# A hybrid convolution, state-space and Fourier block: how the first token tiles are normalised and turned, and how the first quarter of the modulation matrix is loaded

## The chip, the cores and the metric

The kernel runs on one core of one Trainium2 chip. The metric is the device time of one execution in microseconds (us). Before the change three executions took 2059.18, 2054.16 and 2054.33 us; the median is 2054.33 us.

## The reference, cut to what matters

One layer over 512 latent tokens and 256 context tokens of width 2048. What the change touches is the beginning: the modulation vectors, the RMS norm, and the first projection of it.

```python
mod_x = jax.nn.silu(c) @ w_ada[l] + b_ada[l]              # w_ada is 2048 x 6144
sh_x, sc_x, gt_x = jnp.split(mod_x[:, None, :], 3, axis=-1)
mod_c = jax.nn.silu(c_ctx) @ w_ada[l] + b_ada[l]
sh_c, sc_c, gt_c = jnp.split(mod_c, 3)
h_x = _rmsnorm(x, g_pre[l]) * (1 + sc_x) + sh_x           # x is 512 x 2048
h_c = _rmsnorm(ctx, g_pre[l]) * (1 + sc_c) + sh_c         # ctx is 256 x 2048
parts_x = _split_proj(h_x @ w_in[l])                      # w_in is 2048 x 14336
u_c = h_c @ w_in[l][:, U_OFF:U_OFF + W_SSM]
```

All of it is float32. The convolution branch, the state-space scan, the Fourier branch, the gates and the output projection follow from `parts_x` and `u_c` and are the same before and after.

## The kernel before, in words

The kernel is written out by hand for each engine, with semaphores between them; every engine works its list in order. After a head of some 160 us it is a long run of matrix products on TensorE. Float32 matrices are split into a rounded high part and a low part (ScalarE copies the high part, VectorE subtracts), and each product is high by high, high by low and low by high.

A piece of `w_in` in the long run is 128 columns wide, so its row pieces are 512 B.

The head computes `h_x` and `h_c`, transposed (channels on the partitions), and the first four column blocks of the `u` projection. It loads on the queue of SyncE, in this order (lines 378 to 387): the two condition rows, x in four tiles of 128 tokens (1 MB each), then 32 units of `w_ada`, 1 MB each as two transfers of 512 KB (line 367), through a ring of four places. Unit n waits until unit n - 4 has been used. Behind units 6 and 7 of each eight comes one 512 KB unit of `w_in` (line 374), and behind units 8 and 9 one tile of ctx each. The 32 units are four quarters of eight: quarter q holds columns 512q to 512q + 511 of the shift part and of the scale part, all 2048 rows, 256 rows in each unit. A row piece of a unit is 2 KB long.

TensorE, per quarter: `ada` (line 586) multiplies a unit by the two condition vectors and accumulates two short rows in PSUM; after eight units ScalarE copies the rows out (`rows_cp`, line 989), `cols` (line 593) turns them to columns and VectorE's `columns` (line 1434) forms scale and shift for four blocks of 128 channels. VectorE's `modulate` (lines 1452 and 1456) applies them to a turned block, ScalarE's `high` and VectorE's `low` (line 1465) split the result. `x_piece` (lines 633 to 637) and `c_piece` (650 to 653) are the products of one block with its part of `w_in`. The first `ada` of a quarter waits for `columns` of the quarter before (`col_rd`), since both use one PSUM bank.

The norm of the latent tokens (lines 1010 to 1022): ScalarE squares and sums the four tiles, one square root serves all four, VectorE finishes the reciprocal root (lines 1362 and 1354 to 1358), and ScalarE scales all four tiles in place. Then TensorE turns twelve of the sixteen channel blocks (`early_turn`, line 602, four transposes of 128x128 each) in groups of three between `ada` units 3 to 6, and ScalarE copies each to `xT`. The other four blocks are turned in the last quarter. The ctx tiles are squared, scaled and turned later (lines 1027 to 1034 and 620).

VectorE has a second job in the head: the discretisation of the state-space part, on small tiles [128, 64]. It is an exponential of one column (starting at line 1346) and of 64 (1348), the steps for the sine (lines 1366 to 1383), for the cosine (1387 to 1391), `zoh` (1395 to 1409) and `chunk_powers` (1412 to 1425). In the first quarter `zoh` stands ahead of the ctx blocks' `modulate`, and `chunk_powers` behind them, ahead of `columns(1)`.

Of the kernel before, what the change touches and what calls it, by code (L numbers as in the profile page):

```python
# [28 lines left out]
D = 2048  # L29
T = 512  # L30
# [69 lines left out]
def program(nc, x, c, ctx, c_ctx, w_ada, b_ada, g_pre, g_post, w_in, conv_w, lam_re, lam_im, log_dt,  # L100
# [15 lines left out]
    class Region:  # L116
# [5 lines left out]
        def __call__(self, name, shape, dt=F32):  # L122
# [71 lines left out]
    junk = at("junk", [128, D], abr_at + KD // 2 * TC * 4)  # L194
    last4 = (KD - 4) * T * 4
    ring = [at(f"ring{n}", [128, 2, 2, 512], off)
            for n, off in enumerate((hx_at + last4, hxl_at + last4, tab_at, tab_at + 8192))]
# [25 lines left out]
    vrow = r("vrow", [V_END, 128])  # L223
    lam = r("lam", [128, 2, P])
# [3 lines left out]
    assert r.p <= abr_at + KD // 2 * TC * 4  # L228
# [60 lines left out]
                            for name, n in (("ada_in", 4), ("u_out", 4), ("gw_in", 4)))  # L289
# [34 lines left out]
    win = lambda col, n: [(w_in, 0, col, n), (w_in, 1024, col, n)]  # L324
    ph_u = (2, lambda i: [q for j in range(2) for q in win(COL["u"] + 512, (i, 2, j))])
# [245 lines left out]
    def _(pe):  # L571
# [6 lines left out]
        def ada(n):  # L578
            q, r = n // 8, n % 8
            if r == 0 and q:  # L580
                pe.wait_ge(col_rd, q)
            pe.wait_ge(ada_in[n % 4], 32 * (n // 4 + 1))
# [7 lines left out]
        def cols(q):  # L590
            pe.wait_ge(row_cp, q + 1)
            for k in range(4):
# [4 lines left out]
        def early_turn(k):  # L597
            pe.wait_ge(y_done, TT)
            if k >= 4:
                pe.wait_ge(xp_done, k - 3)  # L600
            for t in range(TT):
                last = tr(ac[:, k % 4, t * 128:(t + 1) * 128], xn[:, t, k * 128:(k + 1) * 128], ident[:, :])
            last.then_inc(xp_ps, 1)

        def turn(q, n):
# [4 lines left out]
            if n < 4:  # L610
                pe.wait_ge(y_done, TT)
# [70 lines left out]
        for n in range(8):  # L682
            ada(n)
            if n == 3:
                pe.wait_ge(vec_in, 64)
                tr(ss[:, 1, 0:V_END], vrow[:, :], ident[0:V_END, 0:V_END])
                tr(ss[:, 1, 128:128 + G], drow[:, :, :].rearrange("n l h -> n (l h)"), ident[0:G, 0:G]).then_inc(vec_ps, 1)
            if 3 <= n < 7:
                for k in range(3 * (n - 3), 3 * (n - 2)):
                    early_turn(k)  # L690
        cols(0)
        ada(8)
        ada(9)
        pe.wait_ge(xp_done, EARLY)
        for r in range(4):
            x_piece(0, r, range(4))
            ada(10 + r)
        turn(0, 4)
        ada(14)
        turn(0, 5)  # L700
        for q in range(3):
            if q:
                x_piece(q, 0, range(4))
                ada(8 * q + 12)
                x_piece(q, 1, range(4))
                turn(q, 4)
                ada(8 * q + 13)
                x_piece(q, 2, range(4))
                ada(8 * q + 14)
                turn(q, 5)  # L710
                x_piece(q, 3, range(4))
# [258 lines left out]
    def _(act):  # L970
# [19 lines left out]

        def high(q, n):
# [18 lines left out]
        for t in range(TT):  # L1010
            act.wait_ge(x_in[t], 16)
            st.link(a(junk[:, :], toks[t], ACT.Square, accum_out=small[:, 32 + t:33 + t]))
        act.wait_ge(var_done, 1)
        a(small[:, 46:50], small[:, 40:44], ACT.Sqrt).then_inc(rt_done, 1)
        act.wait_ge(rs_done, 1)
        for t in range(TT):
            cp(toks[t], toks[t], small[:, 52 + t:53 + t]).then_inc(y_done, 1)
        for k in range(EARLY):
            act.wait_ge(xp_ps, k + 1)
            cp(xT[:, k, :], ac[:, k % 4, :]).then_inc(xp_done, 1)  # L1020
            if k == 8:
                hi_first(0)
        hi_first(1)
        rows_cp(0)
        for n in range(4):
            high(0, n)
# [3 lines left out]
        act.wait_ge(var_done, 2)  # L1030
        a(small[:, 50:52], small[:, 44:46], ACT.Sqrt).then_inc(rt_done, 1)
        act.wait_ge(rs_done, 2)
# [264 lines left out]
        act.wait_ge(var_done, 3)  # L1297
# [9 lines left out]
    def _(dve):  # L1307
# [4 lines left out]
        st.link(v.memset(ss[:, 2, :], 0.0))  # L1312
# [30 lines left out]
        dve.wait_ge(ssm_in, 48)  # L1343
        a0, a1, a2, a3, a4, a5, a6, a7 = [z[:, :] for z in zt]
        lre, lim = lam[:, 0, :], lam[:, 1, :]
        exp(a7[:, 0:1], ldt[:, :], a1[:, 0:1], a2[:, 0:1], a3[:, 0:1], a4[:, 0:1], ei[:, 0:1])
        link(ts_(a0, lre, a7[:, 0:1], None, ALU.mult))
        exp(a6, a0, a1, a2, a3, a4, ei[:, :])

# [16 lines left out]
        link(ts_(a0, lim, a7[:, 0:1], None, ALU.mult))  # L1366
        nearest(a1, a0, 1.0 / math.pi)
        link(stt(a2, a1, -3.140625, a0, ALU.mult, ALU.add))
        link(stt(a2, a1, -9.67502593994140625e-4, a2, ALU.mult, ALU.add))
        link(stt(a2, a1, -1.509957990978376432e-7, a2, ALU.mult, ALU.add))  # L1370
        nearest(a3, a1, 0.5)
# [593 lines left out]
```

## Time and profile before

| what | value |
|---|---|
| median of three executions | 2054.33 us |
| the profiled execution's own time | 2054.32 us |
| its span, first to last instruction | 2052.5 us |
| TensorE busy | 2008.0 us, 98% of the span |
| TensorE weight loads | 1640.1 us, 80% |
| VectorE busy | 1085.8 us, 53% |
| ScalarE busy | 594.9 us, 29% |
| data moved | 270.72 MB, 132 GB/s over the span |

Matrix products are pipelined, so a product's duration (392 ns for one of 512 columns) is longer than the step from one to the next. Positions in time below are microseconds from the start of the span. In a row of the timeline the first number is the start, the second the length of the whole group, and the bracket at the end the idle time of the engine just before it and what ended it. A float32 product that isn't a transpose is recorded as two instructions.

### The profile page before, as it was taken

The numbers are of one execution on the slowest core, as the hardware profiler recorded it, in microseconds if no ns is written. First come the engines' busy times: TensorE is split into PE (matmuls) and PEld (weight loads), VectorE is DVE, ScalarE is ACT, GpSimd is POOL, SyncE is SP. The second block draws the span as 40 slices with busy tenths as digits, with TensorE's granted clock in tenths as the row PEclk, the third lists the DMA queues.
The fourth block names the chain that finished last, engine by engine and source line by source line (L and its number), as shares of the span: only waits on it lengthen the run. The fifth ranks groups of instructions, "written<-read, shape, count | busy, mean of one in ns | idle before, by whom it ended". The sixth has DMA issues, their size and how long they took to land.

```text
span 2052.5 us, 26821 instructions
## 1 busy us (share of the span) xinstructions
PE 2008.0 (98%) x10086; PEld 1640.1 (80%) x10086; DVE 1085.8 (53%) x1640; ACT 594.9 (29%) x845; POOL 27.4 (1%) x16
## 2 busy tenths in 40 slices
PE   4999999999999999999999999999999999999998
PEld 1568888888888888888888888888888888888886
DVE  4545799999998645554433434332433333333325
ACT  5325343334343322222222222222322222222222
POOL 0003100000000000000000000000000000000000
PEclk9999999999999999999999999999999999999999
DMA  9963544344344544443334444443233333334423
GB/s 361 366 199 116 168 106 109 102 106 108 102 108 112 179 129 133 125 138 108 100 94 138 134 123 138 133 133 104 73 92 102 93 97 97 93 101 154 173 99 128
DMA packets 384079, 270.72 MB, mean 132 GB/s; under 512 B 24820, under 2 KB 349916, under 8 KB 382164
## 3 DMA queue, kind: packets, MB, share of 16 engines
q1 hardware_dynamic: 373728, 265.61, 42.0%
q10 hardware_dynamic: 10292, 4.33, 1.5%
q8 instruction: 36, 0.59, 0.1%
q14 instruction: 23, 0.19, 0.0%
HBM read 251.81 MB, written 18.09 MB: 131 GB/s over the span
## 4 chain that ended last, share of the span: by engine, by line
PE 93%; DVE 3%; ACT 2%; DMA 1%; issue 1%; SPq 0%; ACTq 0%; DVEq 0%
PE ac L753 25%; PE ac L757 25%; PE ac L754 24%; PE ac L938 1%; PE ac L939 1%; PE ac L937 1%; PE ss L815 1%; PE ss L586 1%; PE ss L939 1%; PE ss L938 1%; PE ss L937 1%; PE ac L633 1%; PE ac L634 1%; PE ac L637 1%; DMA wslot<-w_in 1%; PE ss L808 1%
## 5 line engine op out<-in xcount | busy, mean ns | idle before, releaser
L1557 DVE TENSOR_TENSOR wlo<-wslot,whi 128x1024 fp32r<-128x1024 f32 x309 | 378.3, 1224 | 643.4 <-ACT whi L973 639.3
L973 ACT ACTIVATE whi<-wslot 128x1024 fp32r<-128x1024 f32 x327 | 346.9, 1061 | 1244.3 <-PE ac L757 1042.8
L753 PE MATMUL ac<-hxh,whi 128*128 128x512 f32 x1664 | 651.9, 392 | 0.0
L754 PE MATMUL ac<-hxl,whi 128*128 128x512 f32 x1664 | 647.8, 389 | 0.0
L757 PE MATMUL ac<-hxh,wlo 128*128 128x512 f32 x1664 | 411.2, 389 | 0.9 <-DVE wlo L1557 0.9
L753 PEld LDWEIGHTS ac<-hxh,whi 128*128 128x128 f32 x1664 | 312.4, 188 | 67.4 <-issue 2.9
L757 PEld LDWEIGHTS ac<-hxh,wlo 128*128 128x128 f32 x1664 | 312.3, 188 | 66.1 <-DVE wlo L1557 1.3
L754 PEld LDWEIGHTS ac<-hxl,whi 128*128 128x128 f32 x1664 | 312.4, 188 | 63.8
L753 PE MATMUL ac<-bah,whi 128*128 128x512 f32 x384 | 149.4, 389 | 0.0
L754 PE MATMUL ac<-bal,whi 128*128 128x512 f32 x384 | 149.4, 389 | 0.0
L757 PE MATMUL ac<-bah,wlo 128*128 128x512 f32 x384 | 94.8, 389 | 0.0
L753 PEld LDWEIGHTS ac<-bah,whi 128*128 128x128 f32 x384 | 72.1, 188 | 15.0
L757 PEld LDWEIGHTS ac<-bah,wlo 128*128 128x128 f32 x384 | 72.1, 188 | 15.0
L754 PEld LDWEIGHTS ac<-bal,whi 128*128 128x128 f32 x384 | 72.1, 188 | 14.9
L753 PE MATMUL ac<-b2nd,whi 128*128 128x512 f32 x192 | 74.8, 390 | 0.0
L754 PE MATMUL ac<-b2nd,whi 128*128 128x512 f32 x192 | 74.7, 389 | 0.0
L1776 DVE TENSOR_TENSOR gtm<-ac,gsig 128x512 f32<-128x512 f32 x32 | 22.1, 691 | 85.7 <-PE ac L757 85.7
L586 PE MATMUL ss<-ring,cs 128*2 128x512 f32 x256 | 38.0, 675 | 24.0 <-DMA ring<-w_ada 20.7
L1732 DVE SCALAR_TENSOR_TENSOR gacc<-gwt,cs,gacc 128x256 f32<-128x256 f32 x120 | 57.8, 481 | 3.4
L937 PE MATMUL ac<-whi,mhi 128*128 128x512 f32 x128 | 50.2, 392 | 0.0
L939 PE MATMUL ac<-whi,mlo 128*128 128x512 f32 x128 | 49.8, 389 | 0.0
L938 PE MATMUL ss<-wlo,mhi 128*128 128x512 f32 x128 | 49.8, 389 | 0.0
(359 smaller groups left out, 2076.0 us busy)
## 6 DMA issues: line engine op xcount, KB each, us to landing
wslot<-w_in SPq DMA_DIRECT2D x224, 512.0 KB, 3.8
ring<-w_ada SPq DMA_DIRECT2D x64, 512.0 KB, 8.4
gwt<-w_ada SPq DMA_DIRECT2D x128, 128.0 KB, 2.5
wslot<-w_out SPq DMA_DIRECT2D x32, 512.0 KB, 3.6
wslot<-proj_a SPq DMA_DIRECT2D x16, 512.0 KB, 4.1
wslot<-proj_b SPq DMA_DIRECT2D x16, 512.0 KB, 4.1
wslot<-proj_c SPq DMA_DIRECT2D x16, 512.0 KB, 3.9
xn<-x SPq DMA_DIRECT2D x4, 1024.0 KB, 9.6
```

Source lines behind the costliest of these rows:

```text
L586: last = mm(ss[p:p + 2, 2, :], cs[:, 2 * r + kk, :], ring[n % 4][:, kk, h, :], start=(r == 0), stop=(r == 7))
L633: mm(ac[:, m, :], w, hxh[:, k, :], start=(k == 0), stop=False)
L753: mm(ac[:, bank, :], w, xh, start=(v == 0 and q == 0), stop=False)
L754: mm(ac[:, bank, :], w, xl, start=False, stop=False)
L757: last = mm(ac[:, bank, :], wlo[:, s, q * 128:(q + 1) * 128], rhs(v * UNIT + q)[0], start=False, stop=(v == nu - 1 and q == UNIT - 1))
L937: mm(acc[:, t, :], mh, wh, start=(kk == 0), stop=False)
L938: mm(acc[:, t, :], mh, wl, start=False, stop=False)
L939: last = mm(acc[:, t, :], ml, wh, start=False, stop=(kk == KD - 1))
L973: cp = lambda o, i, scale=1.0: nc.scalar.activation(o, i, ACT.Copy, scale=scale)
L1557: tt(wlo[:, s, :], wslot[:, s, :], whi[:, (U0[k] + j) % 2, :].bitcast(F32), ALU.subtract)\
L1732: stt(gacc[:, :], gwt[:, r % 4, :], cs[:, r, 0:1], gacc[:, :], ALU.mult, ALU.add)\
L1776: tt(o if br == 0 else gtm2[:, :], ac[:, (2 * j + 1) % 4, :], gsig[:, :], ALU.mult)\
```

## The change

The latent tiles are no longer scaled in place. For each tile VectorE makes a diagonal matrix of its 128 reciprocal roots as soon as that tile's sum is there, and TensorE multiplies the raw tile by it, which scales and turns at once (a float32 product in place of a transpose). Root and reciprocal are done per tile. The twelve blocks of one tile are three PSUM banks of four blocks, in rotation over five banks. The remaining four channel blocks are scaled in place by ScalarE, behind the ctx tiles.

The first quarter of `w_ada` is loaded in two halves of its columns: unit n below 8 holds 512 rows of 256 columns, so that four units complete the first half; a row piece is 1 KB. Two ring places are added, used once each. `cols`, `columns` and the row copy of the first quarter are done per half. The first two `w_in` units come behind units 3 and 7, both ctx tiles behind unit 7. The order of the first quarter on TensorE, ScalarE and VectorE is written anew; sine, cosine and `zoh` move behind other work of VectorE.

```diff
+    diag = at("diag", [128, TT, 128], abr_at + L * H * 4)
+            for n, off in enumerate((hx_at + last4, hxl_at + last4, tab_at, tab_at + 8192,
+                                     hx_at + 4 * T * 4, hx_at + 8 * T * 4))]
+    slot = lambda n: n if n < 6 else (n - 6 if n < 8 else n % 4)
...
SyncE, ada_unit(n)
-            if n >= 4:
-                sp.wait_ge(ada_used, n - 3)
+            if n >= 6:
+                sp.wait_ge(ada_used, n - 3 if n > 9 else n - (5 if n < 8 else 1))
+            if n < 8:
+                half, r = n // 4, n % 4
+                for h in range(2):
+                    sp.dma_start(halves(n)[:, :, h, :],
+                                 w_ada[r * 512:(r + 1) * 512, h * D + half * 256:h * D + (half + 1) * 256]
+                                 .rearrange("(k p) c -> p k c", p=128)).then_inc(ada_in[slot(n)], 16)
+                return
...
         for n in range(32):
             ada_unit(n)
-            if n % 8 >= 6:
+            if n in (3, 7):
+                first_unit(n // 4)
+            if n == 7:
+                for t in range(CT):
+                    sp.dma_start(cn[:, t, :], ctx[0, t * 128:(t + 1) * 128, :]).then_inc(c_in, 16)
+            if n > 8 and n % 8 >= 6:
                 first_unit(n // 8 * 2 + n % 2)
-            if n in (8, 9):
-                sp.dma_start(cn[:, n - 8, :], ctx[0, (n - 8) * 128:(n - 7) * 128, :]).then_inc(c_in, 16)
...
TensorE
+        def early_turn(t):
+            pe.wait_ge(y_done, t + 1)
+            for g in range(PARTS):
+                n = t * PARTS + g
+                if n >= 5:
+                    pe.wait_ge(xp_done, n - 4)
+                for k in range(4):
+                    c0 = (4 * g + k) * 128
+                    last = mm(early_bank(n)[:, k * 128:(k + 1) * 128], xn[:, t, c0:c0 + 128], diag[:, t, :],
+                              start=True, stop=True)
+                last.then_inc(xp_ps, 1)
...
+        early_turn(0)
+        early_turn(1)
+        early_turn(2)
+        ada(0)
+        early_turn(3)
+        for n in range(1, 4):
             ada(n)
+        pe.wait_ge(vec_in, 64)
+        tr(ss[:, 1, 0:V_END], vrow[:, :], ident[0:V_END, 0:V_END])
+        tr(ss[:, 1, 128:128 + G], drow[:, :, :].rearrange("n l h -> n (l h)"), ident[0:G, 0:G]).then_inc(vec_ps, 1)
+        cols(0, range(2))
+        ada(4)
+        ada(5)
+        pe.wait_ge(xp_done, TT * PARTS)
+        x_piece(0, 0, range(4))
+        ada(6)
+        ada(7)
+        x_piece(0, 1, range(4))
+        cols(0, range(2, 4))
         ada(8)
         ada(9)
+        x_piece(0, 2, range(4))
+        ada(10)
+        x_piece(0, 3, range(4))
         turn(0, 4)
+        ada(11)
+        turn(0, 5)
+        ada(12)
+        c_piece(0, 0)
+        ada(13)
         ada(14)
+        c_piece(0, 1)
+        ada(15)
+        c_piece(0, 2)
+        cols(1)
+        c_piece(0, 3)
+        for n in range(16, 20):
+            ada(n)
(quarters 1 to 3 as before)
...
ScalarE
+        token_square(0)
+        token_root(0)
+        token_square(1)
+        token_root(1)
+        token_square(2)
+        token_root(2)
+        early_out(0)
+        token_square(3)
+        token_root(3)
+        for t in range(1, TT):
+            early_out(t)
+        rows_half(0)
+        hi_first(0)
+        high(0, 0)
+        high(0, 1)
+        rows_half(1)
         hi_first(1)
+        high(0, 2)
+        high(0, 3)
         act.wait_ge(c_in, 32)
...
         for t in range(TT, TT + CT):
             cp(toks[t], toks[t], small[:, 52 + t:53 + t]).then_inc(y_done, 1)
+        for t in range(TT):
+            o = xn[:, t, EARLY * 128:]
+            last = cp(o, o, small[:, 52 + t:53 + t])
+        last.then_inc(y_done, 1)
         high(0, 4)
...
VectorE
+        def token_diag(t):
+            token_scale(t, 1, t + 1)
+            dve.wait_ge(rs_done, t + 1)
+            ts_(diag[:, t, :], ident[:, :], small[:, 52 + t:53 + t], None, ALU.mult).then_inc(y_done, 1)
+        token_diag(0)
+        token_diag(1)
+        dve.wait_ge(ssm_in, 48)
+        exp(a7[:, 0:1], ldt[:, :], a1[:, 0:1], a2[:, 0:1], a3[:, 0:1], a4[:, 0:1], ei[:, 0:1])
+        token_diag(2)
+        token_diag(3)
...
         for q in range(4):
+            columns(q, range(2 if q == 0 else 4))
+            modulate(q, 0)
             if q == 0:
                 lo_first(0)
-            columns(q)
-            modulate(q, 0)
             low(q, 0)
             modulate(q, 1)
             low(q, 1)
-            if q:
+            if q == 0:
+                sines()
+                columns(0, range(2, 4))
+            else:
                 lo_first(2 * q)
             modulate(q, 2)
+            if q == 0:
+                lo_first(1)
             low(q, 2)
             modulate(q, 3)
             low(q, 3)
-            lo_first(2 * q + 1)
-            if q == 0:
-                token_scale(TT, CT, 2)
-                zoh()
+            if q:
+                lo_first(2 * q + 1)
+            else:
+                token_scale(TT, CT, TT + 1)
             for n in range(4, 6):
                 modulate(q, n)
                 low(q, n)
             if q == 0:
+                cosines()
+                zoh()
                 chunk_powers()
```

## Rows read from the trace of the kernel before

**Rows 1.** The page, busy time of each engine.

```profile
PE 2008.0 (98%) x10086; PEld 1640.1 (80%) x10086; DVE 1085.8 (53%) x1640; ACT 594.9 (29%) x845; POOL 27.4 (1%) x16
```

**Rows 2.** Stretches of the head: busy time per engine, granted clock, DMA share, GB/s.

```profile
49.00:52.00 3.00, 2.46 (x10) 0.66 (x11) 1.61 (x4) 1.26 (x2) 0.00 (x0) 0.50 1.00 386
...
79.00:84.00 5.00, 4.57 (x36) 2.70 (x37) 3.54 (x9) 2.21 (x3) 0.00 (x0) 1.00 0.63 201
80.00:100.00 20.00, 20.00 (x128) 11.95 (x121) 8.93 (x15) 5.05 (x7) 0.00 (x0) 1.00 0.94 339
100.00:120.00 20.00, 20.00 (x134) 12.83 (x134) 8.39 (x15) 5.73 (x8) 0.00 (x0) 1.00 0.94 328
```

**Rows 3.** The DMA view of the stretch from 17 to 76 us.

```profile
DMA packets 11106, 22.99 MB, mean 390 GB/s; under 512 B 669, under 2 KB 669, under 8 KB 10847
```

**Rows 4.** The timeline of TensorE, 0 to 150 us.

```profile
18.94 1.89 PE L586 MATMUL ss<-ring,cs 128*2 128x512 f32 x8 [15.50 <-DMA ring<-w_ada]
...
31.43 2.82 PE L602 MATMUL ac<-ident,xn 128*128 128x128 f32 x12 [1.00 <-ACT xn L973]
...
41.52 1.53 PE L602 MATMUL ac<-ident,xn 128*128 128x128 f32 x12
...
49.54 1.89 PE L586 MATMUL ss<-ring,cs 128*2 128x512 f32 x8 [1.84 <-DMA ring<-w_ada]
...
55.73 1.04 PE L586 MATMUL ss<-ring,cs 128*2 128x512 f32 x8
...
59.64 1.04 PE L586 MATMUL ss<-ring,cs 128*2 128x512 f32 x8
...
79.43 1.04 PE L586 MATMUL ss<-ring,cs 128*2 128x512 f32 x8 [2.95 <-DVE vmod L1434]
...
84.60 1.90 PE L586 MATMUL ss<-ring,cs 128*2 128x512 f32 x16
86.43 0.50 PE L633 MATMUL ac<-hxh,whi 128*128 128x512 f32 x1
```

**Rows 5.** The timeline of VectorE, 0 to 150 us.

```profile
8.02 0.15 DVE L1330 TENSOR_SCALAR zt<-ldt 128x1 f32<-128x1 f32 x1 [1.45 <-DMA ldt<-ssm_log_dt]
...
12.22 0.25 DVE L1347 TENSOR_SCALAR zt<-lam,zt 128x64 f32<-128x64 f32 x1
...
30.93 0.19 DVE L1387 TENSOR_SCALAR zt<-zt 128x64 f32<-128x64 f32 x1
...
34.09 0.22 DVE L1391 TENSOR_TENSOR zt<-zt,zt 128x64 f32<-128x64 f32 x1
...
58.98 0.22 DVE L1395 TENSOR_TENSOR ZN<-zt,zt 128x64 f32<-128x64 f32 x1
...
62.90 0.23 DVE L1409 TENSOR_TENSOR ZN<-zt,zt 128x64 f32<-128x64 f32 x1
...
73.81 0.22 DVE L1412 TENSOR_TENSOR zt<-zt 128x64 f32<-128x64 f32 x1
...
79.16 0.22 DVE L1434 TENSOR_TENSOR vmod<-ss,vecs 128x8 f32<-128x8 f32 x2
```

**Rows 6.** The timeline of ScalarE, 0 to 150 us.

```profile
7.86 1.91 ACT L1012 ACTIVATE junk<-xn 128x2048 f32<-128x2048 f32 x1 [1.51 <-DMA xn<-x]
...
23.70 7.68 ACT L973 ACTIVATE xn<-xn,small 128x2048 f32<-128x2048 f32 x4 [1.11 <-DVE small L1358]
32.58 0.60 ACT L973 ACTIVATE xT<-ac 128x512 f32<-128x512 f32 x1 [1.20 <-PE ac L602]
...
53.49 1.90 ACT L1029 ACTIVATE junk<-cn 128x2048 f32<-128x2048 f32 x1
...
59.10 3.90 ACT L973 ACTIVATE cn<-cn,small 128x2048 f32<-128x2048 f32 x2 [1.09 <-DVE small L1358]
```

**Rows 7.** The timeline of TensorE, 255 to 262 us: float32 products that are no transposes.

```profile
257.07 3.71 PE L815 MATMUL ss<-U,VT 128*128 128x96 f32 x32
```

**Rows 8.** A stretch of the long run of products, same columns as rows 2.

```profile
1500.00:1600.00 100.00, 100.00 (x443) 82.84 (x442) 36.40 (x43) 23.51 (x26) 0.00 (x0) 1.00 0.33 95
```

More of the change, by code:

```diff
@@ L324, in program @@
     win = lambda col, n: [(w_in, 0, col, n), (w_in, 1024, col, n)]
+    halves = lambda n: ring[slot(n)][:, :, :, :].rearrange("p a b c -> p (a b c)")\
+        .rearrange("p (k h c) -> p k h c", k=4, h=2)
     ph_u = (2, lambda i: [q for j in range(2) for q in win(COL["u"] + 512, (i, 2, j))])
@@ L580, in ada @@
             if r == 0 and q:
-                pe.wait_ge(col_rd, q)
-            pe.wait_ge(ada_in[n % 4], 32 * (n // 4 + 1))
+                pe.wait_ge(col_rd, q + 1)
+            pe.wait_ge(ada_in[slot(n)], filled(n))
+            if n < 8:
+                r = n % 4
+                for kk in range(4):
+                    for h in range(2):
+                        p = 64 * (kk % 2) + 32 * h
+                        last = mm(ss[p:p + 2, 2 + n // 4, 0:256], cs[:, 4 * r + kk, :], halves(n)[:, kk, h, :],
+                                  start=(r == 0 and kk < 2), stop=(r == 3 and kk > 1))
+                last.then_inc(ada_used, 1)
+                return
             for kk in range(2):
@@ L588, in ada, with cols @@
             last.then_inc(ada_used, 1)
-        def cols(q):
-            pe.wait_ge(row_cp, q + 1)
-            for k in range(4):
+        def cols(q, ks=range(4)):
+            if q or ks[0]:
+                pe.wait_ge(col_rd, q + 1 if q else 1)
+            pe.wait_ge(row_cp, q + 2 if q else ks[0] // 2 + 1)
+            for k in ks:
                 last = mm(ss[:, 2, 4 * k:4 * k + 4], rows[:, k * 128:(k + 1) * 128],
@@ L595, in cols, with early_bank @@
             last.then_inc(col_ps, 1)
[L597 to L603, printed above, removed]
+        PARTS = EARLY // 4
+        def early_bank(n):
+            return (ac[:, n % 5, :] if n % 5 < 4 else ss[:, 0, :])
+        def early_turn(t):
[9 more added lines that the diff above has]
+                last.then_inc(xp_ps, 1)
         def turn(q, n):
@@ L610, in turn @@
             if n < 4:
[L611 removed]
+                pe.wait_ge(y_done, TT + CT + 1)
                 k = 4 * q + n
@@ L680, in p0_c @@
             last.then_inc(p0_ps, 1)
-        for n in range(8):
-            ada(n)
[L684 to L691, printed above, removed]
+        early_turn(0)
[4 more added lines that the diff above has]
+        for n in range(1, 4):
+            ada(n)
+        pe.wait_ge(vec_in, 64)
[10 more added lines that the diff above has]
+        cols(0, range(2, 4))
         ada(8)
         ada(9)
[L694 to L697, printed above, removed]
+        x_piece(0, 2, range(4))
+        ada(10)
+        x_piece(0, 3, range(4))
         turn(0, 4)
-        ada(14)
-        turn(0, 5)
-        for q in range(3):
-            if q:
[L703 to L711, printed above, removed]
+        ada(11)
[3 more added lines that the diff above has]
+        ada(13)
+        ada(14)
+        c_piece(0, 1)
[5 more added lines that the diff above has]
+            ada(n)
+        for q in range(1, 3):
+            x_piece(q, 0, range(4))
+            ada(8 * q + 12)
+            x_piece(q, 1, range(4))
+            turn(q, 4)
+            ada(8 * q + 13)
+            x_piece(q, 2, range(4))
+            ada(8 * q + 14)
+            turn(q, 5)
+            x_piece(q, 3, range(4))
             ada(8 * q + 15)
@@ L989, in rows_cp, with rows_half @@
             cp(rows[:, :], ss[:, 2, :]).then_inc(row_cp, 1)
+        def rows_half(half):
+            act.wait_ge(ada_used, 4 * half + 4)
+            cp(rows[:, half * 256:(half + 1) * 256], ss[:, 2 + half, 0:256]).then_inc(row_cp, 1)
         def high(q, n):
```

123 lines of the change are left out of this document (61 added, 62 removed).

## The prediction

> **What bounds the kernel now.** The page comes first: TensorE is busy for 2008.0 us of 2052.5 [rows 1]. The change touches only the first 85 us or so, and behind the head TensorE simply works its list, so whatever the head gains or loses arrives at the end one for one. The question is what sets the start of the long unbroken stretch. The timeline of TensorE gives it: at 86.43 us the first product of the second quarter starts, and the stretches behind it show TensorE busy 20.00 of 20 us [rows 4, 2]. I call that moment S. The order behind S is the same before and after.
>
> Three things could hold S. The DMA view shows a stream that never pauses from 17 to 76 us, at 390 GB/s [rows 3]; only from 79 to 84 us does it fall to 201 GB/s [rows 2], when it already has a lead. VectorE's timeline shows a chain of small steps, `chunk_powers`, that begins at 73.81 right behind the last ctx block and ends at 79.16, where `columns(1)` starts; TensorE stands idle for 2.95 us and is released by that at 79.43 [rows 5, 4]. Then come two `ada` and two `c_piece`, two more `ada` from 84.60, and S. So S is `columns(1)` plus 7.3 us: VectorE's list binds, with the stream close behind.
>
> **The stream as a floor.** The total loaded up to unit 19 is the same before and after: 28 MB of the 1 MB pieces (x 4, units 20, `w_in` 2, ctx 2), only the order differs. One such piece takes 1.049/0.390 = 2.69 us. Unit 0 is the fifth and was used at 18.94 [rows 4], so piece p is there at 18.94 + 2.69 (p - 5). In the new order that is 27.0 for unit 3, 31.0 and 33.7 for units 4 and 5, 36.4 and 39.1 for 6 and 7, 45.8 for ctx, 48.5 for unit 8, 51.2, 53.9 and 56.6 for 9 to 11, 68.7 for unit 15 and 80.8 for unit 19. S needs `ada(19)`, about 1 us. S can't be before 81.8, and the change can't gain more than 86.4 - 81.8 = 4.6 us, however early TensorE starts.
>
> **The change part by part.**
>
> Removed: ScalarE's scaling in place of the four x tiles, 7.68 us [rows 6], and 48 transposes, which took 1.53 us for twelve at the shorter durations and 2.82 us at first [rows 4]. Added: 48 float32 products. The nearest row is sixteen such products of 96 columns in 3.71 us, 0.23 each [rows 7], against 0.13 for a transpose. 48 of them are 11.1 us, or 22 us if they run as slowly as the first units did (1.89 us for a unit against 1.04) [rows 4]. All lie in a time in which TensorE was waiting for loads. The Trainium skill's page "TensorE: Matmul & The Clock Gate", section "Terms", says that transpose mode is four times faster for float32. By it a product would be about 0.5 us and the 48 would be 24 us, where the two rows give a factor of 1.8.
>
> The early walk, at the shorter durations: the first square starts at 7.86 and takes 2.1 us with its sum [rows 6]; root and diagonal follow, so products start at about 13. Between the second and the third diagonal VectorE has the one-column exponential, 12.22 - 8.02 = 4.2 us [rows 5], which puts the third at about 21.5 and, through ScalarE's list, the fourth at 26. The twelve copies on ScalarE are 0.6 us each [rows 6] and cost nothing beyond the wait for banks. `early_turn(3)` ends at about 30, `ada(1)` to `ada(3)` at 33, the first half's `columns` at 35, `x_piece(0, 0)` runs from 37.5 to 40.5, `ada(6)` ends at 41.5. Before, the first `x_piece` began at 51.43. So TensorE starts 14 us earlier, but this buys only what the stream lets it keep. Unit 8 waits for `ada(6)`; its request must be out before the ctx tiles are through, by about 44. The margin is 2 to 3 us.
>
> The middle: `x_piece(0, 1)` until 45.5, then nothing until unit 8 at 48.5. On VectorE `sines` (25 small steps; 14 such took 34.31 - 30.93 = 3.4 us, so 6.1) [rows 5] lies between `low(0, 1)` and the second `columns`, which puts `high(0, 3)` on ScalarE at about 50.4. The ctx squares stand behind it in ScalarE's list. From the first ctx square to the end of the scaling it was 63.0 - 53.5 = 9.5 us before [rows 6], so both ctx tiles are ready at 60, about when `x_piece(0, 3)` ends. New behind it on ScalarE: four copies of the remaining x columns, 4 x 0.6 = 2.4 us, ahead of `high(0, 4)`, for which VectorE's `low` waits. The last `low` of the quarter ends at about 66, against 73.8.
>
> What is late next: VectorE now has cosine, `zoh` and `chunk_powers` there, 3.4 + 4.1 + 5.4 = 12.9 us (34.31 - 30.93, 63.13 - 58.98, 79.16 - 73.81) [rows 5], where before only the last stood. 66 + 12.9 gives `columns(1)` at 79.0, TensorE released at 79.3: where it was. The 7.8 us won on the ctx blocks are given back to steps that earlier filled gaps.
>
> Behind the release: before, two `c_piece` and four `ada`, 7.0 us (86.43 - 79.43). In the new order all four `c_piece` of the quarter are done by then, by about 74 (unit 15 at 68.7, then 1.0 + 1.6 + 0.8 + 1.6), and only four `ada` remain: 3.9 us at 0.97. S would be 83.2, a gain of 3.2. But TensorE will have stood idle from 74 to 79.3. After the sparse time before 49.54 an `ada` took 1.89 us, and the granted clock was 0.50 from 49 to 52, the lower of its levels, 1.2 GHz; after an idle time of 2.95 us at 79.43 it took 1.04 and the clock stayed 1.00 [rows 4, 2]. An idle time of 5 us is nearer to the first, so I take three of the four at 1.89: 79.3 + 5.7 + 1.0 = 86.0. Gain 0.4.
>
> Smaller row pieces: eight units have pieces of 1 KB. The stretch of 512 B pieces moved 95 GB/s at a share of 0.33, 288 GB/s at full share [rows 8]; the stream of 2 KB pieces reaches 390 [rows 3]. For 8.4 MB that bounds the cost between nothing and 7.6 us; I take 2 us, as 1 KB lies between. The floor then is 83.8, still ahead of 86.0: it costs nothing in the forecast. The Trainium skill's page "DMA: Bandwidth & Descriptors", section "Specifications", gives 512 B as the smallest transfer at line rate. By it this term is nil, and the floor stays at 81.8.
>
> The two ring places: used once each, they keep the stream fed until unit 8. No further cost. Unit 20 waits for `ada(16)`, about 81 instead of 80.4; it lands by about 86 and is wanted at S + 3. No cost. The rest of the chain (tables, `late_unit`) hangs on TensorE and moves with S.
>
> **Sum.** S moves from 86.4 to 86.0. The profiled execution took 2054.32 us, practically the median 2054.33; minus 0.4 gives 2053.9. What this measurement can tell from no change is about 0.3%, 6.2 us, that is 2048.2 to 2060.5.
>
> **The rivals.**
>
> 1. *The clock holds and S goes to the floor.* Real products keep TensorE busier from 13 us on, and the 5 us idle time doesn't lower the clock. S is then 81.8 to 83.8, the time 2049.7 to 2051.7; 2050.9 from the walk. For it: the 2.95 us without a fall [rows 4]. Against it: clock 0.50 after a sparse stretch [rows 2]. Chance 0.18.
>
> 2. *The turning products are too slow and the stream breaks: slower.* If the 48 products cost 0.46 each, by the lower clock or by themselves, they end 11 us later and the `ada`s around them run at 1.89. `ada(6)` then ends at about 53 to 55, not 41.5; it decides from 44 on. Unit 8 is asked for up to 10 us too late, every landing behind it moves as much: unit 10 at 64, ctx blocks' `low` at about 74, 12.9 us on top, `columns(1)` at 87.5, S at 91.5 to 94. That is +5 to +8, 2059 to 2062, typically 2061. For it: the first units' durations of 1.89 and the first transposes at 2.82 [rows 4]. Against it: twelve transposes fell to 1.53 within 10 us of steady work [rows 4]. Chance 0.10.
>
> 3. *The middle runs at the lower clock.* The idle time from 45.5 to 48.5 and the waits for units 8 to 10 bring the clock down; two `x_piece`s take 4.3 us (55.73 - 51.43) instead of 2.9 (59.64 - 56.77) [rows 4], and the ctx blocks, the 12.9 us and S move by 2 to 4 us: 2055.5 to 2058. Chance 0.20.
>
> 4. *The chain or the stream isn't what holds S at all*, so the 14 us early start is kept in part: over 6 us faster. Rows 3 speak against it. Chance 0.04.
>
> The forecast itself, within 2 us of 2053.9, has 0.48. The range 2050.0 to 2059.5 leaves out about 2 in 10: the lower end of the floor, the upper of rival 2, and rival 4. Faster by over 0.3% is rival 4, 0.04; slower by over 0.3% is most of rival 2 and a little unforeseen, 0.09; the rest, 0.87, is no difference.
>
> **What the profile would show.** Right: the turning products start near 13 us and `x_piece(0, 0)` at 37 to 40; DMA without a pause to 80 us; `columns(1)` within 2 us of 79, released by VectorE's small steps; TensorE idle 4 to 6 us ahead of it; four `ada` of which the first take 1.8 to 1.9 us; S at 84 to 88; an unchanged time from S to the end. Wrong if `columns(1)` comes before 76 or after 83, if DMA stands still near 45 us, or if the stretch behind S changes its length.

## The result, and the profile after

The kernel after takes 2059.10 us, the median of 13 executions (2058.58 to 2061.07), beside 2054.93 us for 13 of the kernel before (2053.72 to 2059.18): a ratio of 1.0018, 95% interval 1.0011 to 1.0025. It is 4.2 us slower, where I had forecast 0.4 us faster. That is less than the 0.3% I took as the limit of the measurement, but the interval is clear of 1, so it has to be explained.

The profiled execution took 2059.96 us. Its page, to be held against [rows 1]:

```profile
span 2058.2 us, 27076 instructions
PE 2015.3 (98%) x10198; PEld 1652.2 (80%) x10198; DVE 1092.7 (53%) x1665; ACT 590.1 (29%) x849; POOL 25.0 (1%) x16
```

The timeline of TensorE, kernel after, answers to [rows 4]:

```profile
12.74 6.51 PE L640 MATMUL ac<-diag,xn 128*128 128x128 f32 x32 [9.40 <-DVE diag L1477]
...
20.06 2.94 PE L640 MATMUL ac<-diag,xn 128*128 128x128 f32 x24
...
36.43 1.88 PE L607 MATMUL ss<-ring,cs 128*2 128x256 f32 x16 [1.97 <-DMA ring<-w_ada]
38.24 0.80 PE L672 MATMUL ac<-hxh,whi 128*128 128x512 f32 x1
...
51.61 1.04 PE L614 MATMUL ss<-ring,cs 128*2 128x512 f32 x8 [3.35 <-DMA ring<-w_ada]
54.22 1.89 PE L614 MATMUL ss<-ring,cs 128*2 128x512 f32 x8 [1.57 <-DMA ring<-w_ada]
56.04 0.80 PE L672 MATMUL ac<-hxh,whi 128*128 128x512 f32 x1
...
61.50 0.50 PE L672 MATMUL ac<-hxh,whi 128*128 128x512 f32 x1
...
64.37 0.60 PE L659 MATMUL ss<-ident,cn 128*128 128x128 f32 x4
...
82.84 5.31 PE L614 MATMUL ss<-ring,cs 128*2 128x512 f32 x32 [4.44 <-DVE vmod L1532]
...
88.08 0.50 PE L672 MATMUL ac<-hxh,whi 128*128 128x512 f32 x1
```

The last row is S, the moment the prediction is about: 88.08 us, against 86.43 before and 86.0 forecast. The picture in front of it is the one forecast, with `columns(1)` 3.5 us late. VectorE's chain of small steps (timeline of VectorE, its first and last row and what follows; compare [rows 5]) is 12.9 us long, as summed:

```profile
69.61 0.19 DVE L1467 TENSOR_SCALAR zt<-zt 128x64 f32<-128x64 f32 x1
...
82.22 0.42 DVE L1522 COPY ZN<-ZN 128x448 f32<-128x448 f32 x1
82.56 0.22 DVE L1532 TENSOR_TENSOR vmod<-ss,vecs 128x8 f32<-128x8 f32 x2
```

S accounts for 1.65 us of the 5.7 by which the two profiled spans differ (2058.2 - 2052.5). The medians lie only 4.2 us apart, because the profiled execution of the kernel after is 0.9 us above its median and that of the kernel before 0.6 us under its own. The other 4 us between the spans arise far behind S. Two rows, one of GpSimd and one of VectorE, show where; first the kernel before:

```profile
189.27 4.54 POOL L562 TENSOR_TENSOR wlo<-wslot,whi 128x1024 fp32r<-128x1024 f32 x1 [6.03 <-ACT whi L973]
189.25 2.29 DVE L1539 TENSOR_TENSOR B<-B,Brw 128x2048 f32<-128x2048 f32 x1
```

and the kernel after:

```profile
190.90 2.56 POOL L581 TENSOR_TENSOR wlo<-wslot,whi 128x1024 fp32r<-128x1024 f32 x1 [6.04 <-ACT whi L1030]
186.71 2.29 DVE L1642 TENSOR_TENSOR Brw<-Brw,q 128x2048 f32<-128x2048 f32 x1 [7.51 <-ACT Brw L1030]
191.24 4.37 DVE L1644 TENSOR_TENSOR B<-B,Brw 128x2048 f32<-128x2048 f32 x1
```

Both kernels run the same two instructions here: GpSimd makes a low part of `w_in`, and VectorE takes the last step of the table B. Whichever starts second lasts some 2.1 us longer. Before, VectorE is first by 0.02 us and GpSimd pays (4.54 instead of 2.40 us), which costs nothing: before_order below, in which GpSimd takes its 2.38 us alone, needs as long from there to the end (1893.00 against 1892.95 us). After, GpSimd is first by 0.34 us and VectorE pays (4.37 instead of 2.29 us). For this the Trainium skill, page "SBUF — State Buffer", section "Who interferes with whom", has the rule: a VectorE instruction with two inputs in SBUF contends with a GpSimd instruction that reads SBUF, and issue order decides which one blocks until the other is done. The rows agree with it, and it was there to be read beforehand. So was the effect itself, in the trace of the kernel before. VectorE's first instruction on 128x256 elements starts 0.09 us behind GpSimd's first low part and lasts 2.58 us; the next one of that shape lasts 0.41:

```profile
159.55 2.40 POOL L562 TENSOR_TENSOR wlo<-wslot,whi 128x1024 fp32r<-128x1024 f32 x1 [158.07 <-ACT whi L973]
159.64 2.58 DVE L1519 TENSOR_TENSOR Ar<-Ar 128x256 f32<-128x256 f32 x1
162.15 0.41 DVE L1520 TENSOR_TENSOR Ai<-Ar,Ai 128x256 f32<-128x256 f32 x1
```

VectorE's delay goes on, because the store of B stands in SyncE's list ahead of the next unit of `w_in`. Timeline of SyncE, kernel before and then kernel after:

```profile
191.57 0.55 SPq L472 DMA_DIRECT2D tab_dram<-B  x1
192.17 0.67 SPq L458 DMA_DIRECT2D wslot<-w_in  x1
```

```profile
195.64 0.55 SPq L491 DMA_DIRECT2D tab_dram<-B  x1
196.23 0.67 SPq L477 DMA_DIRECT2D wslot<-w_in  x1
```

That unit is 4.06 us later, of which 1.6 us are the later head (GpSimd's first low part is at 161.17 instead of 159.55) and 2.4 us are new. ScalarE's high parts behind it are as late (203.05 against 198.98), and near 219 us TensorE runs dry and comes back at the lower clock. Timeline of TensorE, then the stretches view (columns as in [rows 2]), kernel after:

```profile
219.15 0.47 PE L831 MATMUL ac<-hxh,whi 128*128 128x512 f32 x1 [2.50 <-ACT whi L1030]
...
220.01 0.63 PE L831 MATMUL ac<-hxh,whi 128*128 128x512 f32 x1
```

```profile
210.00:230.00 20.00, 17.50 (x92) 15.00 (x91) 13.21 (x31) 5.09 (x9) 4.83 (x2) 0.91 0.79 234
200.00:240.00 40.00, 37.49 (x203) 32.28 (x202) 19.04 (x46) 14.43 (x28) 10.67 (x5) 0.96 0.56 164
```

The kernel before has in the same 40 us:

```profile
200.00:240.00 40.00, 39.76 (x218) 34.16 (x217) 23.01 (x50) 15.94 (x32) 12.39 (x5) 1.00 0.55 160
```

TensorE is busy for 2.27 us less, and a clock of 0.96 over 40 us is, as an estimate, 1.6 us of lost work: 3.9 us together, of the 4.1 us that the table below gives for this part.

**One way to read every run.** I cut each profiled span in three: up to S; from S to GpSimd's first low part (near 160 us); and from there to the end. "Held" says that VectorE's last step of B was the one to wait. The three parts belong to one profiled execution, whose own time stands beside the median of all executions of the kernel; where the two differ, the parts explain the first.

| kernel | S | S to GpSimd's first | from there to the end | held | profiled | median |
|---|---|---|---|---|---|---|
| before | 86.43 | 73.12 | 1892.95 | no | 2054.32 | 2054.93 |
| after | 88.08 | 73.09 | 1897.03 | yes | 2059.96 | 2059.10 |
| before_held | 86.02 | 73.14 | 1897.34 | yes | 2058.26 | 2060.85 |
| after_order | 87.40 | 74.96 | 1892.94 | no | 2057.14 | 2056.78 |
| before_order | 89.65 | 74.65 | 1893.00 | no | 2059.11 | 2057.88 |
| before_warm_order | 85.88 | 73.12 | 1893.00 | no | 2053.82 | 2053.82 |
| after_wide_order | 85.58 | 75.12 | 1893.10 | no | 2055.60 | 2054.58 |
| after_turn_order | 88.50 | 73.13 | 1893.87 | no | 2057.32 | 2056.29 |
| after_fill_order | 87.52 | 75.81 | 1892.77 | no | 2057.91 | 2057.70 |
| after_wide_fill_order | 84.89 | 74.65 | 1892.66 | no | 2053.97 | 2055.83 |
| before_fill_order | 83.22 | 73.11 | 1893.27 | no | 2051.35 | 2051.48 |
| before_fill | 82.74 | 74.71 | 1893.65 | no | 2052.89 | 2051.82 |
| full_fill_order | 80.93 | 75.92 | 1893.05 | no | 2051.70 | 2051.81 |

The last part has two values: 1892.7 to 1893.9 without the hold, and 1897.0 or 1897.3 with it. full_fill_order apart, the middle part is 73.1 wherever the granted clock was 1.00 from 140 to 150 us, and 1.5 to 2.7 longer where it was 0.83 to 0.90 there (TensorE has two gaps near 140 us). The clock falls there in some executions and not in others: before_fill and before_fill_order have the same head and differ in it. full_fill_order's first two parts aren't comparable: two `ada` and two pieces are exchanged around S.

### The profile page after: what moved, and what is told of

It reads as the page before. It is cut to its first block, busy times and chain, and to the rows that moved or that the text cites. A ratio compares the mean times of both kernels' runs of the same rounds, so it can differ in the third digit from the quotient of the medians.

```text
span 2058.2 us, 27076 instructions
## 1 busy us (share of the span) xinstructions
PE 2015.3 (98%) x10198; PEld 1652.2 (80%) x10198; DVE 1092.7 (53%) x1665; ACT 590.1 (29%) x849; POOL 25.0 (1%) x16
## 4 chain that ended last, share of the span: by engine, by line
PE 92%; DVE 3%; DMA 2%; SPq 1%; ACT 1%; issue 1%; DVEq 0%; ACTq 0%
PE ac L810 25%; PE ac L814 25%; PE ac L811 24%; PE ac L996 1%; PE ac L995 1%; PE ac L994 1%; PE ss L872 1%; PE ss L995 1%; PE ss L996 1%; PE ss L994 1%; SPq L377 1%; PE ss L614 1%; DMA ring<-w_ada 1%; PE ac L672 1%; PE ac L673 1%; PE ac L676 1%
## 5 line engine op out<-in xcount | busy, mean ns | idle before, releaser
L995 PE MATMUL ac<-wlo,mhi 128*128 128x512 f32 x128 | 49.8, 389 | 0.0
```

The costliest lines, as they stand in the source:

```text
L995: mm(acc[:, t, :], mh, wl, start=False, stop=False)
```

## The experiments

All runs but before_held and before_fill share one edit that fixes the order of the two engines (GpSimd's fifth low part waits for VectorE's B), so that the head can be read by itself; the label says so with "order". Ratios are to the kernel before on the same chip, each from 11 executions.

### The order alone, in either direction

after_order, and the same edit in the kernel before, before_order:

```diff
 for j in range(10):
+    if j == 4:
+        pool.wait_ge(bb_done, 1)
     lo(0, 0, j)
```

> The changed kernel; GpSimd's fifth wlo subtraction waits until VectorE's last B step is done, so that the two can't run at once near 191 us. Theory 1 (of the 4.1 us, 1.65 come from the head, S at 88.1 instead of 86.4, and the rest from VectorE's B step being held behind GpSimd, 4.37 us long instead of 2.29, with an idle TensorE and a lower clock behind it): B step back to 2.3 us, TensorE idle before the product at 219 us below 0.5 us, time 2055.5 to 2056. Rival (the rest comes from something else behind the head, loads or fetches): B step 2.3 us but time stays at 2058.5 to 2059.5.

> The kernel before with the same added wait of GpSimd. Theory 1: nothing changes in the executions in which VectorE came first anyway (2054), and the executions at 2057.5 disappear: all executions within 1 us of 2054. Rival (the 2057.5 executions have another cause): they stay, in about a third of the executions.

before_held, the kernel before with the opposite order:

```diff
+dve.wait_ge(w_lo, UFIRST + 5)
 tt(B1[:, :, :], B1[:, :, :], Brw2[:, :, :], ALU.add).then_inc(bb_done, 1)
```

> The kernel before; VectorE's last B step waits until GpSimd's fifth wlo subtraction is done, which puts it about 2.4 us later, as being held did. Theory 1: TensorE idle for 2 to 3 us near 217 us, time 2057 to 2058.5, that is the slower executions of the kernel before made permanent. Rival: the delay is absorbed, 2054 to 2055.

after_order: 2056.78 us (2055.10 to 2058.04), 1.0002 [0.9993, 1.0011]. No execution of it is as slow as the fastest of the kernel after. before_held: 2060.85 us (2057.54 to 2063.27), 1.0021 [1.0012, 1.0030]. The delay of B alone, put into the kernel before, brings 4.4 us in the last part of the table, and taking it out of the kernel after removes 4.1 us there. Both medians lie above what I expected, and they show the 4 us less exactly. after_order is only 2.3 us below the kernel after: in its profiled execution the first 160 us are 1.2 us longer (162.36 against 161.17), at a clock of 0.84 from 140 to 150 us. before_held is 5.7 us above the kernel before beside it (2055.16), but its profiled execution is a fast one, 2.6 us under its median; what the slower ones lose besides, no profile shows. GpSimd's and VectorE's rows of after_order, then VectorE's and TensorE's of before_held:

```profile
194.79 2.40 POOL L581 TENSOR_TENSOR wlo<-wslot,whi 128x1024 fp32r<-128x1024 f32 x1 [8.74 <-DVE B L1646]
192.42 2.29 DVE L1646 TENSOR_TENSOR B<-B,Brw 128x2048 f32<-128x2048 f32 x1
```

```profile
191.38 2.29 DVE L1540 TENSOR_TENSOR B<-B,Brw 128x2048 f32<-128x2048 f32 x1 [2.54 <-POOL wlo L562]
...
217.61 0.77 PE L774 MATMUL ac<-hxh,whi 128*128 128x512 f32 x1 [2.97 <-ACT whi L973]
```

So neither engine is slow when it runs alone, and a delay of B by 2.5 us through a plain wait costs the same 4 us. With the order fixed in both kernels, the kernel after (2056.78) isn't slower than the kernel before (before_order, 2057.88); beside the kernel before without the wait (2055.16) the difference isn't clear of the scatter. before_order missed: 2057.88 us, from 2053.96 to 2059.78, 1.0005 [0.9996, 1.0014]. I had expected its slower executions to be held ones and to vanish. They stayed without any hold, so the spread of the kernel before comes from elsewhere. Its profile shows from where (TensorE; compare the 1.04 us at 79.43 in [rows 4]):

```profile
79.84 1.89 PE L588 MATMUL ss<-ring,cs 128*2 128x512 f32 x8 [2.96 <-DVE vmod L1436]
...
84.51 1.77 PE L588 MATMUL ss<-ring,cs 128*2 128x512 f32 x8
```

The same idle time (2.95 us there) that left the clock alone in one execution brought it down in this one (0.50 from 79.4 to 86 us), and S went to 89.65.

### Is the spread the clock?

before_warm_order fills TensorE's idle time with products of the identity, which nobody reads:

```diff
+def keep(n, bank):
+    for _ in range(n):
+        mm(ss[:, bank, 0:128], ident[:, :], ident[:, :], start=True, stop=True)
...
+if q == 0 and r == 1:
+    pe.wait_ge(ht_done, 6)
+    keep(12, 3)
```

(and five and eight more at the two gaps near 140 us).

> The kernel before, with GpSimd's wait for VectorE's last step of B, and with products of the identity with itself (128 by 128, read by nobody) in TensorE's idle time: 12 ahead of the products of unit 16 (where it stood idle for 2.95 us near 79 us), 5 and 8 at the two later gaps near 140 us. Question: with the wait alone the executions still spread from 2053.96 to 2059.78 us. Theory A: TensorE's clock falls after those idle stretches in some executions; with the engine busy all executions lie within 2.0 us of each other, with a median of 2053.5 to 2055, and the profile shows no half-clock stretch between 79 and 160 us. Rival B: the spread has another cause; it stays over 4 us and the median is 2055 to 2058. Rival C: the extra products themselves delay the list, a median over 2056 with a spread under 2 us, GpSimd's first low part then starting after 162.

2053.82 us, from 2053.11 to 2055.06, 0.9990 [0.9981, 0.9999]. The spread is 1.95 us, where the 27 executions of the kernel before beside it span 6.3 (2053.69 to 2060.01) and 12 of them lie above 2056. Theory A holds, and the granted clock is 1.00 in every stretch from 79 to 160 us. All three gaps were filled at once, so how much each gives isn't shown. Timeline of TensorE:

```profile
75.77 2.84 PE L686 MATMUL ss<-ident 128*128 128x128 f32 x24
78.88 1.04 PE L588 MATMUL ss<-ring,cs 128*2 128x512 f32 x8 [0.27 <-DVE vmod L1448]
```

### The row pieces of 1 KB

after_wide_order is after_order with the first eight units in 2 KB pieces; the scale and shift of the first quarter are then made from other columns than the reference's.

```diff
-sp.dma_start(halves(n)[:, :, h, :],
-             w_ada[r * 512:(r + 1) * 512, h * D + half * 256:h * D + (half + 1) * 256]
+sp.dma_start(ring[slot(n)][:, :, h, :],
+             w_ada[n * 256:(n + 1) * 256, h * D:h * D + 512]
```

> The changed kernel with GpSimd's wait; the first eight units keep their place, size and order, but their row pieces are 2 KB (256 rows of 512 columns each), so that the first quarter's scale and shift are not the reference's. Theory 2 (1 KB pieces make the stream late, 349 instead of 387 GB/s, by some 2.5 us, and that delays the ctx blocks and the columns): unit 8 used at 48.5 to 49.5 instead of 51.6, second-quarter columns at 79.5 to 81, S 1.5 to 2.5 us earlier than with the wait alone (87.4). Rival (the clock decides S, not the stream): DMA at 387 GB/s but S within 1 us of 87.4.

2054.58 us (2052.80 to 2055.60), 0.9994 [0.9985, 1.0003]: 2.2 below after_order, which ran on another chip; the two intervals overlap. The profile carries the finding: unit 8 is used at 49.68 instead of 51.92 in after_order, and S is at 85.58 instead of 87.40, 1.8 earlier. The DMA view of 17 to 76 us, kernel after and then after_wide_order; [rows 3] is that of before:

```profile
GB/s 349 349 348 348 350 346 354 383 344 351 346 349 349 346 349 356 411 439 372 417 392 380 387 389 386 389 382 389 389 385 387 296 353 376 301 296 305 374 356 378
DMA packets 14059, 21.45 MB, mean 364 GB/s; under 512 B 618, under 2 KB 8141, under 8 KB 13798
```

```profile
DMA packets 10805, 22.42 MB, mean 380 GB/s; under 512 B 652, under 2 KB 652, under 8 KB 10544
```

The forty slices are 1.475 us each. While the 1 KB pieces arrive, up to 40 us, 15 of 16 show 344 to 356 GB/s; from 48 to 62 us, with 2 KB pieces, they show 380 to 389. That is a tenth less for the size of the piece. The Trainium skill, page "DMA: Bandwidth & Descriptors", section "Specifications", has line rate from 512 B up; these rows go against that.

### Products or transposes

after_turn_order turns the twelve blocks with transposes again, and leaves their scaling out.

```diff
-last = mm(early_bank(n)[:, k * 128:(k + 1) * 128], xn[:, t, c0:c0 + 128], diag[:, t, :],
-          start=True, stop=True)
+last = tr(early_bank(n)[:, k * 128:(k + 1) * 128], xn[:, t, c0:c0 + 128], ident[:, :])
```

> The changed kernel with GpSimd's wait; the 48 products with the diagonal are transposes (the x tiles stay without their scaling in those twelve blocks). Theory (the turning products are hidden under the loads): the turning ends 2 to 4 us earlier, x_piece(0,0) and S move by less than 0.7 us, time as with the wait alone, 2055 to 2058. Rival (the products hold the head): S 2 us or more earlier.

2056.29 us (2055.92 to 2057.71), 1.0002 [0.9993, 1.0011], and S at 88.50: nothing gained. The turning didn't end 2 to 4 us earlier either, but at 29.5 us, against 29.3 with the products in after_order. The shorter transposes leave TensorE idle for 3.41 us ahead of 19.95, and from 23 to 30 us its granted clock is 0.54, where it is 1.00 in after_order. Twelve transposes then take 2.85 us, as long as twelve products at the full clock. So the products that the change is named after cost no time here.

### VectorE's steps, in both kernels

after_fill_order moves cosine and `zoh` ahead of the ctx blocks, into time in which VectorE only waits:

```diff
 token_scale(TT, CT, TT + 1)
+cosines()
+zoh()
...
-    cosines()
-    zoh()
     chunk_powers()
```

> The changed kernel with GpSimd's wait, and VectorE's cosine and zoh steps put ahead of the ctx blocks, where VectorE stood idle for 7.3 us, instead of behind them. Theory 2 (VectorE's steps behind the ctx blocks set S): second-quarter columns start at 76 to 78 instead of 82.6, S at 83 to 84.5 instead of 88.1, time 3.5 to 5 us below the changed kernel with the wait alone, 2051 to 2052. Rival (the load stream sets S): columns early, but S at 86 or later, gain below 2 us.

2057.70 us (2054.96 to 2059.32), 1.0007 [0.9998, 1.0016]: the rival, no gain. `columns(1)` starts at 77.12, as early as expected, but now the loads are late, and S is at 87.52. Timeline of TensorE, `ada(17)` to `ada(19)`:

```profile
80.29 1.04 PE L616 MATMUL ss<-ring,cs 128*2 128x512 f32 x8 [0.71 <-DMA ring<-w_ada]
82.98 1.83 PE L616 MATMUL ss<-ring,cs 128*2 128x512 f32 x8 [1.66 <-DMA ring<-w_ada]
85.71 1.89 PE L616 MATMUL ss<-ring,cs 128*2 128x512 f32 x8 [0.89 <-DMA ring<-w_ada]
```

before_fill_order does the like in the kernel before, with `chunk_powers`:

```diff
     zoh()
+    chunk_powers()
 for n in range(4, 6):
     modulate(q, n)
     low(q, n)
-if q == 0:
-    chunk_powers()
```

> The kernel before with GpSimd's wait, and VectorE's chunk_powers put ahead of the ctx blocks. Theory 2 (VectorE's steps hold S in the kernel before too): second-quarter columns at 74.5 to 76 instead of 79.2, TensorE no longer idle for 2.95 us ahead of the first unit of the second quarter, S at 83 to 84, no fall of the clock near 80, time 2050.5 to 2052.5. Rival (the stream holds S): S within 1 us of 86.4.

2051.48 us (2050.75 to 2052.55), 0.9981 [0.9972, 0.9990]: as theory 2 expected, and faster than both kernels, with `columns(1)` at 74.79, S at 83.22 and a spread of 1.8 us. before_fill is the same without GpSimd's wait:

> The kernel before with VectorE's chunk powers ahead of the first blocks of ctx, and no wait on GpSimd: is the order of the two engines near 190 us left to chance here? With the wait this edit gave 2051.48 us. Theory A: in the kernel before VectorE's last step of B starts 0.02 us ahead of GpSimd's low part, and the edit moves both by the same amount, since both follow from TensorE's list; the time is 2051.5 (2050.7 to 2052.6), B's step takes 2.3 us and GpSimd's instruction 4.5. Rival B: the order turns over; B's step takes over 4 us, and the time is 2055.6, 4.1 more. Rival C: it falls now one way, now the other, and the executions stand in two groups some 4 us apart.

2051.82 us (2050.34 to 2052.89), 0.9978 [0.9969, 0.9987]. Here the order stayed as it was, by 0.02 us (GpSimd 187.18 and 4.54 us long, VectorE 187.16 and 2.29), so the wait isn't needed for the gain. The idle time of 2.95 us is gone. Timeline of TensorE, before_fill:

```profile
75.42 1.04 PE L586 MATMUL ss<-ring,cs 128*2 128x512 f32 x8
...
80.62 2.19 PE L586 MATMUL ss<-ring,cs 128*2 128x512 f32 x16
82.74 0.49 PE L633 MATMUL ac<-hxh,whi 128*128 128x512 f32 x1
```

### Everything undone, and the best of both

after_wide_fill_order joins the three edits of the kernel after (order, 2 KB pieces with the other columns, VectorE's steps).

> The kernel after with all three things that the runs so far charge it with undone at once: GpSimd's wait for the last step of B, first units in pieces of 2 KB lines (so the scale and shift of columns 0 to 511 are made from other columns than the reference's), and VectorE's cosines and chunk steps ahead of the first blocks of ctx. The wait alone gave 2056.78 us, wait and wide pieces 2054.58, wait and moved VectorE work 2057.7. Theory A: the wide pieces bring the loads forward, the moved work lets columns follow them, and what is left is the stream; GpSimd's first low part starts near 158 and the time is 2051 to 2052.5. Rival B: the stream still ends the head with no gain from the moved work: 2054 to 2055. Rival C: the moved VectorE work makes the blocks of ctx late and costs what it did with narrow pieces (0.9 us more than the wait alone): 2055 to 2056.

2055.83 us (2053.97 to 2057.48), 1.0001 [0.9992, 1.0010]: by the time, rival C. By its profile, S is 84.89 and set by loads (1.68 and 1.66 us of idle time ahead of the last two `ada`). S is earlier than in after_wide_order (85.58), and yet the median is higher. The profiles can't settle that: this one is of the fastest of eleven executions (2053.97), that of after_wide_order of the slowest (2055.60), and these two times lie the same way as S. What its slower executions lose stays open.

full_fill_order keeps the early products and the six places, but loads whole units of 2 KB pieces (all columns right), has VectorE's steps in its gaps, and puts `x_piece(1, 0)` and `x_piece(1, 1)` between `ada(17)` and `ada(19)`:

```diff
-if n < 8:
-    half, r = n // 4, n % 4
...
-    return
...
 for q in range(4):
+    if q == 0:
+        sines()
+        cosines()
     columns(q)
...
     token_scale(TT, CT, TT + 1)
+    zoh()
```

> A version meant to be the fastest: the changed kernel with the early products with the diagonal, the six ring places and GpSimd's wait, but the first quarter in whole units again (2 KB pieces), sine, cosine and zoh in VectorE's idle times ahead of the columns and of the ctx blocks, and the first two x_pieces of the second quarter set between its loads. If VectorE's tail, the small pieces and the idle wait for the loads are what costs: first x_piece of the second quarter at 77 to 80, end of the second quarter 5 us earlier than before, time 2047 to 2051. Rival (the stream is the floor of the head): not below 2052.

2051.81 us (2051.00 to 2053.78), 0.9985 [0.9976, 0.9994]. That is above the 2047 to 2051 expected and under the rival's 2052, so neither holds as stated; the first x_piece of the second quarter, at 80.93, is also later than the 77 to 80 expected. The time is the same as that of before_fill_order, an edit that moves one step. In this combination, turning early and the two extra places buy nothing beyond what the place of VectorE's steps gives.

## Why the prediction was wrong, point by point

**"Behind the head TensorE simply works its list, so whatever the head gains or loses arrives at the end one for one": the step that failed.** It priced everything from S to the end at nothing. I had listed "an unchanged time from S to the end" as a sign of being right; it changed by 4.1 us (1897.03 against 1892.95 from GpSimd's first low part on). The list stayed the same, but a pair of instructions on VectorE and GpSimd start 0.02 us apart in it, and their order turned over. after_order and before_held show that this decides the 4 us. S doesn't enter: in the runs of the kernel before, B's step starts 29.61 to 29.71 us after GpSimd's first low part, whatever S is, and in the kernel after and three runs from it 30.06 to 30.10. GpSimd's own start is at 29.72 or 29.73 in both kernels. The 0.36 us come from the step two ahead, which starts 0.10 us after ScalarE's copy in the one (184.72 against 180.78 + 3.84) and 0.46 us in the other (186.71 against 182.41 + 3.84). With cosine and `zoh` moved forward it is 0.11 again (after_fill_order 188.51, the copy ending at 188.40), so it goes with the order of VectorE's list in the head; by which way, no run shows, and why this step starts later stays open. That the measured 2059.10 still lies between the 2050.0 and 2059.5 that I gave is luck: that end was set by rivals 2 and 3, and neither of them has the 4.1 us.

**S: 86.0 forecast, 88.1 measured.** Three terms stand out, besides a walk through the loads that was about 1 us too early: even with 2 KB pieces unit 8 came at 49.68 (48.5) and `columns(1)` at 80.14 (79.0).

- *Smaller pieces: mis-sized by being set to nothing.* My estimate was 2 us, and the forecast let it vanish behind VectorE's chain. But the chain begins when the ctx blocks are through, and they hang on the loads. Unit 8 came at 51.61 (forecast 48.5), unit 9 at 54.22 (51.2), `x_piece(0, 3)` ended near 64.3 (60), the ctx blocks' `low` at 69.7 (66), `columns(1)` stood at 82.56 (79.0). So what the loads lost went through. after_wide_order gives the pieces' part as 2.2 us at unit 8 and 1.8 us of S: the estimate of 2 us was right, and setting it to nothing was the fault.
- *The clock in the middle: rival 3, right in kind, though not forecast.* After 3.35 and 1.57 us of waiting for units 8 and 9, `x_piece(0, 2)` ran at 0.63 us a product instead of 0.39. The rival's place and cause are what the rows show. Its 2 to 4 us are not: one piece was slow, not two, and it took 4.5 us (56.04 to 60.53) instead of the 2.9 of the next, 1.6 us more.
- *The four `ada` at the lower clock: right, but too dear.* I put 6.7 us from release to S, with 5.7 of them at the lower clock; it was 5.24 (88.08 - 82.84). The granted clock was 0.63 from 83 to 84 us, 0.50 from 84 to 86, 0.66 from 86 to 87 and 1.00 behind it, so only some 3 us ran at the lower level.

**The stream's floor was too low.** I had unit 19 there at 80.8, or 2 us later with small pieces, from a stream that never pauses. In the new order it slackens. Stretches view of 60 to 70 us, before and then after:

```profile
60.00:70.00 10.00, 10.00 (x60) 5.09 (x52) 3.58 (x13) 3.00 (x2) 0.00 (x0) 1.00 1.05 386
```

```profile
60.00:70.00 10.00, 9.88 (x65) 5.46 (x67) 3.56 (x8) 5.36 (x7) 0.00 (x0) 1.00 0.98 342
```

The ring places come free too late: `ada(11)` now stands behind `x_piece(0, 3)` and the first turned ctx block, and unit 15 waits for it. Its request in SyncE's timeline, before and then after, is 5.3 us later:

```profile
60.74 0.88 SPq L367 DMA_DIRECT2D ring<-w_ada  x2
```

```profile
66.00 0.88 SPq L382 DMA_DIRECT2D ring<-w_ada  x2
```

after_fill_order has unit 19 at 85.7 and unit 8 at 51.75, which is 4.9 and 3.25 us behind my walk; after_wide_fill_order has them at 83.9 and 49.58, 3.1 and 1.1 behind. So between the two units some 1.7 to 2 us are lost, whatever the size of the pieces. That the place of `ada(11)` does it is read from these rows; no run moved it. I worked the floor out from landings alone, and never from when the places come free.

**What held.** First turning product at 12.74 (13). 0.245 us a product (2.94 for twelve; 0.23 forecast) against 0.13 for a transpose [rows 4], a factor of 1.9, so these rows go against the factor of four that the Trainium skill gives (page "TensorE: Matmul & The Clock Gate", section "Terms"). Early start and products hidden (after_turn_order). VectorE's chain 12.9 us and the releaser of `ada(16)`. TensorE idle 4.4 us ahead of it (5). The lower clock behind it. In the sum of rival 1, the 2050.9 "from the walk" should be 2051.1 (2054.3 - 3.2); nothing hangs on it. Rival 1, a clock that holds, and rival 2, turning products that break the stream, didn't come; none of the rivals had the mechanism that decided.

## What to carry to other kernels

A long list that is "the same before and after" can still change its length: look in it for pairs of instructions on VectorE and GpSimd that start within some tenths of a microsecond of each other, and ask what waits for each. If only one may be late, fix the order with a semaphore. Small steps of an engine belong into its waits, and not ahead of the step that releases the next stage: one moved step gained 3 to 4 us here (medians of 2051.48 and 2051.82 beside 2055.24 and 2054.62), and the new order of the whole head that was tried on top of it added nothing. A landing time is only as good as the moment at which its buffer is free.

## What was unexpected of the hardware

- VectorE's and GpSimd's elementwise instructions on SBUF don't share the time but take turns, in the pairs shown here. The later one lasted 4.37 instead of 2.29 us, or 4.54 instead of 2.40, with 0.02 us of lead enough to decide.
- The same idle time of 2.95 us on TensorE was followed by a granted clock of 1.00 in one execution and 0.52 (79 to 84 us) in another of the kernel before with GpSimd's wait. Filling it, together with two gaps near 140 us, took the spread from 6.3 to 1.95 us.
- Pieces of 1 KB ran at 344 to 356 GB/s, pieces of 2 KB at 380 to 389, in the same trace.
